# Order of modulation blocks, one queue and one operation's engine in the first attention of a two-block transformer kernel

## The reference, cut to what matters

```
mod = silu(c) @ w_ada + b_ada                     # 2048 -> 6 * 2048: shifts, scales and gates
h   = rms_norm(x) * (1 + scale_m) + shift_m
q, k, v, gates = split(h @ w_in)                  # two attention mixers
p = exp(s - max);  p = p / sum(p)                 # in the first mixer also times a gate per token and head
o = concat(mixer_1, mixer_2) @ w_o
x = x + gate_m * rms_norm(o)
x = x + gate_f * rms_norm(relu(h' @ w_up)^2 @ w_down)
```

## Time and profile before

| | |
|---|---|
| median of 3 runs | 2945.11 us (2944.65 to 2951.2) |
| the profiled execution | 2945.3 us |
| its span | 2943.5 us |
| TensorE matmuls | 2874.3 us busy, 98% of the span |
| VectorE | 1685.7 us, 57% |
| ScalarE | 1264.9 us, 43% |
| GpSimd | 106.4 us, 4% |
| mean granted TensorE clock | 0.987 of full speed |
| fetched and stored | 596.74 MB, mean 203 GB/s |

### The profile page before, as it was taken

One profiled execution on the slowest core, in us unless ns is written; L12 is line 12 of the kernel. 1 busy time (PEld: TensorE's weight loads), 2 busy tenths in 40 slices (PEclk: granted clock), 3 DMA queues, 4 the chain that ended last, 5 costly groups with the idle time before them and its releaser, 6 DMA issues.

```text
span 2943.5 us, 51154 instructions
## 1 busy us (share of the span) xinstructions
PE 2874.3 (98%) x22398; PEld 2650.3 (90%) x22398; DVE 1685.7 (57%) x1509; ACT 1264.9 (43%) x1236; POOL 106.4 (4%) x95
## 2 busy tenths in 40 slices
PE   6999999999999999999999999999999999999999
PEld 5999998899889997899999889999889998899888
DVE  7888787784444454465455644445745544455544
ACT  3334554445334443345343544443345443344433
POOL 0010000000000000000012410000000000000000
PEclk8899999999999999999999999999999999999999
DMA  9999878596556665655451015556555555565553
GB/s 361 387 314 323 271 253 321 191 354 205 191 189 197 188 197 175 206 186 172 162 172 49 10 64 184 197 189 225 172 186 164 194 192 194 188 198 189 183 188 127
DMA packets 300501, 596.74 MB, mean 203 GB/s; under 512 B 12192, under 2 KB 17824, under 8 KB 299808
## 3 DMA queue, kind: packets, MB, share of 16 engines
q1 hardware_dynamic: 294912, 587.83, 59.3%
q10 hardware_dynamic: 5408, 6.23, 0.8%
HBM read 583.80 MB, written 6.29 MB: 200 GB/s over the span
## 4 chain that ended last, share of the span: by engine, by line
PE 87%; DVE 6%; ACT 3%; DMA 2%; issue 2%; POOL 0%; SPq 0%; ACTq 0%; DVEq 0%
PE ps L2475 30%; PE ps L2398 26%; PE ps L3017 9%; PE ps L2586 6%; PE ps L2601 3%; PE ps L3140 2%; DVE wL L1401 2%; DVE ada_acc L1621 2%; PE ps L2898 2%; PE ps L2558 1%; ACT wH L777 1%; DMA raw<-w_up 1%; DMA ada<-w_ada 1%; PE ps L2421 1%; PE ps L2377 0%
## 5 line engine op out<-in xcount | busy, mean ns | idle before, releaser
L1401 DVE TENSOR_TENSOR wL<-raw,wH 128x2048 fp32r<-128x2048 f32 x436 | 1000.7, 2295 | 1071.6 <-ACT wH L777 1067.3
L777 ACT ACTIVATE wH<-raw 128x2048 fp32r<-128x2048 f32 x436 | 837.9, 1922 | 1325.6 <-PE ps L2475 460.7
L2475 PE MATMUL ps<-actH,wH 128*128 128x256 f32 x2816 | 780.5, 277 | 3.2 <-DVE wL L1401 3.2
L2475 PE MATMUL ps<-actL,wH 128*128 128x256 f32 x2816 | 778.4, 276 | 0.0
L2475 PE MATMUL ps<-actH,wL 128*128 128x256 f32 x2816 | 778.3, 276 | 0.0
L2475 PEld LDWEIGHTS ps<-actH,wH 128*128 128x128 f32 x2816 | 529.5, 188 | 6.0 <-issue 3.2
L2475 PEld LDWEIGHTS ps<-actL,wH 128*128 128x128 f32 x2816 | 529.6, 188 | 0.1
L2475 PEld LDWEIGHTS ps<-actH,wL 128*128 128x128 f32 x2816 | 529.4, 188 | 0.0
L2398 PE MATMUL ps<-wH,hidH 128*128 128x512 f32 x1024 | 403.4, 394 | 1.3 <-DVE wL L1401 1.3
L2398 PE MATMUL ps<-wH,hidL 128*128 128x512 f32 x1024 | 400.4, 391 | 0.0
L2398 PE MATMUL ps<-wL,hidH 128*128 128x512 f32 x1024 | 397.4, 388 | 0.0
(11 more groups left out here) (447 smaller groups left out, 3629.7 us busy)
## 6 DMA issues: line engine op xcount, KB each, us to landing
raw<-w_in SPq DMA_DIRECT2D x96, 1024.0 KB, 5.7
ada<-w_ada SPq DMA_DIRECT2D x80, 1024.0 KB, 8.0
raw<-w_up SPq DMA_DIRECT2D x64, 1024.0 KB, 5.3
raw<-w_down SPq DMA_DIRECT2D x64, 1024.0 KB, 5.1
raw<-w_mlp_up SPq DMA_DIRECT2D x64, 1024.0 KB, 5.3
raw<-w_mlp_down SPq DMA_DIRECT2D x64, 1024.0 KB, 5.0
raw<-w_gates SPq DMA_DIRECT2D x48, 1024.0 KB, 5.1
raw<-w_o SPq DMA_DIRECT2D x16, 1024.0 KB, 7.5
```

Source lines behind the costliest of these rows:

```text
L777: nc.scalar.activation(wH[:, s % SPLIT if L[name]["spg"] > 1 else r % SPLIT, :, :], raw[:, slot, :, :], ACT.Copy).then_inc(wh_ready, 1)
L1401: nc.vector.tensor_tensor(wL[:, b, :, :], raw[:, slot, :, :], wH[:, b, :, :].bitcast(F32), ALU.subtract).then_inc(wl_ready, 1)
L2475: ins = nc.tensor.matmul(out, w[:, b, k, cols], v[:, kk, :], start=(kk == 0 and j == 0 and n % 2 == 0), stop=(kk == STEP_K * spg - 1 and j ...
```

## The change

Subblocks 1, 3, 4, 6 and 7 are multiplied by VectorE inside `weights_of`, as 0, 2 and 5 already were; `weigh` and its calls go. VectorE's order changes in three places: conversion (0,3) stands ahead of the compression inputs; block 40 stands ahead of `modulation(9)`, with blocks 41 to 43 behind split (2,0) and 44 and 45 behind split (2,1); and block 67 stands behind split (w_o 0,1) with 68 and 69. SyncE's order follows: blocks 46 and 47 are asked for behind the fetch of step (2,3), ahead of 42 and 43, and 44 and 45 behind the fetch of step (3,0). The order for other r is the same as before.

```diff
-    WIN_ADA = [(0, 1, 1, 1), (1, 1, 3, 4), (1, 1, 0, 1)] + [(2, 1, 0, 1)] * 4 + [(2, 1, 0, 4)]
+    WIN_ADA = [(0, 1, 1, 1), (1, 1, 3, 2), (3, 1, 0, 1)] + [(2, 1, 0, 1)] * 4 + [(2, 1, 0, 4)]
@@ SyncE
                     weight_block(lin("w_in", 0, r, s) + RAW)
+                    if r == 1 and s == 3:
+                        for n in range(NFRONT + 12, NFRONT + 24):
+                            if ada_slot[n] in (2, 3) and ada_before[n] < NFRONT:
+                                ada_block(n)
                     for j in range(used, used + WIN_ADA[r][s]):
                         for n in ada_next[j]:
                             ada_block(n)
                     used += WIN_ADA[r][s]
-                    if r == 2 and s == 0:
-                        for n in range(NFRONT + 12, NFRONT + 24):
-                            if ada_slot[n] in (2, 3) and ada_before[n] < NFRONT:
-                                ada_block(n)
@@ ScalarE
-            def weigh(b):
-
-                if subs[b][0] == "cmp":
-                    return
-                act.wait_ge(weight, [s[0] for s in subs[1:b + 1]].count("full"))
-                for t in range(TT):
-                    for h in range(4):
-                        p = (probs0, probs1)[t][:, b % 2, h, :]
-                        ins = nc.scalar.activation(p, p, ACT.Copy, scale=rsum[:, b % 2, t, h:h + 1])
-                ins.then_inc(probs_ready, 1)
...
                 split(*(("w_in", 0, r + 1, 0) if r < 7 else ("w_o", 0, 0, 0)))
-                weigh(b + 1)
...
             split("w_o", 0, 0, 1)
-            weigh(7)
@@ VectorE, weights_of
-                if kind == "cmp" or b == 0:
-                    link(ins)
-                    for t in range(TT):
-                        p = pcmp[:, t, :, :] if kind == "cmp" else (probs0, probs1)[t][:, b % 2, :, :]
-                        ins = nc.vector.tensor_tensor(p, p, rsum[:, b % 2, t, :].unsqueeze(2).to_broadcast(list(p.shape)), ALU.mult)
-                    ins.then_inc(probs_ready, 1)
-                else:
-                    ins.then_inc(weight, 1)
+                link(ins)
+                for t in range(TT):
+                    p = pcmp[:, t, :, :] if kind == "cmp" else (probs0, probs1)[t][:, b % 2, :, :]
+                    ins = nc.vector.tensor_tensor(p, p, rsum[:, b % 2, t, :].unsqueeze(2).to_broadcast(list(p.shape)), ALU.mult)
+                ins.then_inc(probs_ready, 1)
@@ VectorE, its order
             split("w_in", 0, 0, 2)
+            split("w_in", 0, 0, 3)
             compress_inputs()
-            split("w_in", 0, 0, 3)
...
+            ada_blocks(1)
             modulation(9, 3)
             split("w_in", 0, 2, 0)
-            ada_blocks(4)
+            ada_blocks(1)
 
             for r in range(2, 8):
                 b = r - 2
                 if r > 2:
                     split("w_in", 0, r, 0)
-                ada_blocks(WIN_ADA[r][0])
+                ada_blocks(2)
                 split("w_in", 0, r, 1)
-                ada_blocks(WIN_ADA[r][1])
+                ada_blocks(2 if r == 2 else 1)
                 split("w_in", 0, r, 2)
...
             weights_of(7)
-            ada_blocks(1)
             split("w_o", 0, 0, 1)
-            ada_blocks(2)
+            ada_blocks(3)
             out_low(6)
```

## The result

The changed kernel takes 2955.09 us (median of 8 runs, 2952.61 to 2956.77) against 2945.01 us before (8 runs beside them). The ratio is 1.0033, with a 95% interval of 1.0023 to 1.0043: slower by 10 us, or 0.33%. The forecast was 2950.0 us with a range of 2941 to 2954, so the time lies 1 us outside it, on the side forecast. The profiled execution took 2955.0 us, its span is 2953.2.

The account below looks back on a forecast made before the run. TensorE carries 87% of the chain, so only its waits and half clock in the first attention count. Terms +0.2 - 1.9 + 0.8 + 4.6 + 1.8 - 0.8 = +4.7 us on 2945.3 gave 2950.0 us, range 2941 to 2954.

Parts of the forecast that it names:

- Part 4: Passage into w_o: block 67 behind the split makes block 69, out_low(6) and values(7) late, +4.6 us; half clock behind, +1.8 us.
- Part 2: Blocks and queue in group 2: block 42 lands at 236 us; together with Part 3 up to step (3,0), -1.9 us.
- Part 3: All probabilities weighted on VectorE, not ScalarE: -1.9 us with Part 2 up to step (3,0), then +0.8 us at split (5,0).
- Set 3: VectorE's probability products ahead of split (5,0): the split ends at 329.5 to 329.7 instead of 327.7, +0.8 us.
- Sets 4 and 6: VectorE's probability products there: one split ended 2 us before it was wanted, the other lies ahead of a score wait; 0.
- Set 1: VectorE's probability products ahead of split (3,0): they end at 261.4, step (3,0) starts at 266.4 against 268.26.
- Part 1: r=0, conversion (0,3) ahead of the compression inputs: a 0.80 us wait goes, but step (1,0) comes later, +0.2 us.
- The half clock behind the narrow matmuls of group 3: TensorE at 0.53 clock for 3.5 us from 279.1; half of its 1.65 us counted as gain, -0.8 us.
- The slower rival: Late block 42 leaves no gain in group 2, w_o costs its upper bound (+8): +9 to +11 us, 2955; chance 0.15.

## Why the prediction was wrong

- **Direction and main place: right.** Part 4 forecast that 67 behind the split makes 69's fetch late, that out_low(6) and values(7) stand behind it, and that TensorE stands still for 5.4 us. It was 5.26. The move alone makes as much loss as the whole change (1.0032 against 1.0033), and taking it back leaves none that can be told from the noise (1.0002).
- **Part 4, size.** Forecast +4.6 and +1.8 = +6.4, measured +6.9 in P. The clock is 2.4 of it (forecast 1.8). Left out was what the late block does to SyncE's queue: the reload of x waits for 69, and weight steps and block 70 wait behind it. Where out_low(6) no longer stood in the way, this cost 4.1 us; in the changed kernel it shows nowhere, so it is not what the forecast missed. By the ratio the move of 67 alone costs 9.4 us where P says 6.4 and the forecast 6.4; the interval (5.9 to 13) includes both.
- **Part 2, group 2: the step that failed.** I took 42 to land at 236 us, from the fully loaded queue's rate, and 43 right behind it with no term of its own, so that both were summed at 241.5, and forecast -1.9 up to step (3,0). In the changed kernel 42 landed at 240.4 and 43 at 243.2, in a trace 1.6 us later there, so 42 was 2.8 us later than worked out, and G was +1.8: 3.7 us off. That is most of the 5 us by which the forecast missed (beside it P is 0.5 above, the front 1.7, M 1.1 below). The missing term is the landing of 43. In the kernel with 67 back, the same up to there, 42 landed 2.3 us sooner than forecast, and G was 47.8 us all the same, 3.3 above the 44.5 of the forecast: 43 landed 1.6 us later than the chain allowed, and its sum took 4.48 us in place of 2.74. The order of the queue is most of it (with 46 and 47 put back, 43 lands 4 to 6 us sooner, and G is 4.3 us shorter). But one of the five kernels with 46 and 47 behind has 43 as late as the rest, so the order is not the only cause; what else delays these fetches, and what makes the sum of 43 longer, stays open.
- **The prediction's own signs** said so: step (2,1) was to start near 244 and began at 249.91; step (3,0) behind 268 was to mean a late fetch, and it began at 271.63, or 270.0 without the 1.6 us.
- **A rule weighed there.** The Trainium skill, DMA: Bandwidth & Descriptors, "Queues, rings and completion order": descriptors of one issuer are consumed in ring order. The traces agree: between 150 and 520 us all 97 to 99 fetches of SyncE landed in the order in which they were asked for, in each of the fourteen. The rule gives the order and not the time: by the rate alone 42 would still have landed 2.8 us sooner in the changed kernel.
- **Part 3.** Set 3 was forecast at +0.8 and step (5,0) comes 0.7 us later behind its turning (2.0 against 1.3). Sets 4 and 6 cost nothing, as said. Set 1 depends on whether block 43 is late: about 2 us or nothing.
- **Part 1.** Forecast +0.2. The stretch is 15.4 us after and 15.6 before, and it lies between 14.4 and 15.8 us in the six traces with the order of before, so a difference of 0.2 cannot be read. The wait moved from 0.80 us ahead of step (0,3) to 0.91 us ahead of step (1,0), as forecast. No experiment isolates it.
- **The half clock behind the narrow matmuls of group 3** is gone in the changed kernel (the clock is 1.00 there), against the half of 1.65 us that I had counted; with the 0.7 of set 3 this gives -1.0 for the -1.1 of M. None of the eight traces in which VectorE weighs subblock 1 has that half clock, and five of the six others have it. Why is open, and M as a whole lies between 152.5 and 155.8 us over the traces.
- **The slower rival** gave 2955 us, and had the mechanism (nothing won in group 2, w_o at its upper bound) at a chance of 0.15. It was the case that came, in kind. That its number fits is in part luck: it counted 8 us at w_o, which cost 6.9, and the trace after has 1.7 us more in its front, which the change does not touch.

## What to carry to other kernels

Before moving a step behind another, look up whose buffer it frees: here one sum, moved by 2.3 us of work, delayed a fetch, a copy out of PSUM, a matmul group and a reload, and cost some 9 us. It had filled the time in which VectorE waits for ScalarE's high part; in the changed kernel VectorE stands idle there (1.46 us) and the sum comes behind. The place where an engine waits anyway is the right place for such a step, not behind it. Judge each part of a bundled reorder by itself, and a stretch that waits on fetches by several executions: in this change one line makes the whole loss that can be measured, and all the others together nothing (1.0002).

## What was not expected of the hardware

- Fetches of 1 MB at the same place of the same order landed up to 5 us apart between executions. With kernels alike up to there, block 42 landed 11.8 us after the start of G in one profiled execution and 16.9 in another, and block 43 13.8 us after it in one and 18.5 in another; VectorE's waits for the two were 3.8 us together and 8.5.
- A standstill of TensorE of 5.3 us cost 2.4 us more behind it, as the clock fell to 0.50. 4.45 us of matmuls whose result nobody reads, put inside it, gave that back. Behind the standstill of 4.5 us in the kernel with block 67 moved alone, values(7) took 4.3 us, so 1.8 more than before.
- The half clock also comes and goes far from any change: the same matmuls ran at a granted clock of 0.50 in one trace and at 1.00 in another. Kernels that differ by a few us in one place cannot be compared by the spans of one trace each.
